# A third pair of operand tiles, a raw ring of three, and a copy of the sums' high part in PSUM, in the down projection of a decoder step

## The chip, the cores and the metric

The kernel runs on one core of one Trainium2 chip. The metric is device time in microseconds. Three runs of the kernel before gave a median of 3109.16 us (3107.42 to 3110.7).

## What is computed

One decoder layer for 512 prompt tokens and 8 sample tokens that share weights (T = 520 columns): a mixer (RG-LRU and gated DeltaNet), cross-attention and a SwiGLU, each with a norm before and after. The change is in the last product of the last part:

```python
def swiglu(xn, p):
    return (jax.nn.silu(xn @ p['ffn_w_gate']) * (xn @ p['ffn_w_up'])) @ p['ffn_w_down']
```

D_MODEL is 2048 and D_FF is 5632, so `ffn_w_down` is 44 x 16 blocks of 128 x 128, all in fp32.

## The kernel before

**Split operands.** Each fp32 operand is split into a high part (a copy to fp32r, made by ScalarE) and a low part (the operand minus its high part, made by VectorE). A product is three matmuls: high with high, high with low, low with high.

**Seven products.** The two feed-forward stages use Strassen's scheme: 2 x 2 blocks of weight against 2 x 2 blocks of tokens (halves of 260 columns) in seven products, collected in PSUM banks 0 to 6. Bank 7 is not used by them. A *slab* is a tile of weight: raw blocks A11, A12, A21, A22 for two pairs, `raw[k]` of 128 x 1024. Of it, three blocks are operands as they are (w_hi and w_lo, planes 0 to 5), and four sums (`w_sums`, later `down_sums`, 128 x 1024) give planes 6 to 13. TensorE takes a slab in 7 x 2 x 3 = 42 matmuls of 260 columns (`products`, L3770 to L3791).

**The down phase.** UP = 176 slabs of the up projection come first; then 88 slabs of down, in four parts of 12, 12, 12 and 8 chunks of D_FF (PARTS). A part has eight *units*, one for each 256 output columns; a unit is three slabs in the first three parts and two in the fourth. At a unit's end VectorE adds the seven banks up (`combine`, L2942 to L2954, four instructions), and the result goes to `ffn_out`: copied by ScalarE in the first part (`copy_out`, L1908), added by GpSimd in the second and third (`add_out`, L1028), added by VectorE in the fourth (L3032), where ScalarE also squares and weighs it (`square_out`, L1921 and L1926) and GpSimd adds the squares (L1037). Towards the end of the first three parts, six, six and two of the hidden activations' sets are loaded from memory and split (`set_high_down` L1897, `set_low_down` L3021), in pairs after a slab.

**What each engine does for slab n**, in a fixed order that is the order of the code:

- SyncE loads raw[n % 4] when slab n-4 has its low part (`load_down`, L1134).
- GpSimd makes the sums of slab n in three instructions (`down_sum`, L1016, L1019, L1021) once slab n-2 has its low part; two buffers take turns.
- ScalarE copies the raw blocks (L1880) and then the sums (L1883) to w_hi. `down_high` waits for `w_used >= n - 1`: TensorE must be done with slab n-2, since two tiles take turns.
- VectorE subtracts: L3012 for the raw blocks, L3015 for the sums, and counts `w_low` up.
- TensorE waits for `w_low` and multiplies.

On ScalarE, `first_product` (L1840) follows the high part of the next unit's first slab; on VectorE, `combine` follows the low part of the same slab.

Of the kernel before, what the change touches and what calls it, by code (L numbers as in the profile page):

```python
# [12 lines left out]
P = 128  # L13
# [48 lines left out]
def build(nc, i, o):  # L62
# [32 lines left out]
    with ExitStack() as ctx:  # L95
        def sb(name, shape, dt=F32):
# [12 lines left out]
                       ("qs_rows", 4), ("k_t", NC // 2), ("s_exp", 1), ("os_rows", 1), ("s_o_high", 1), ("xa_root", 1), ("y_copied", Y_TILES)],  # L109
# [6 lines left out]
                       ("s_probs", 1), ("s_spread", 1), ("s_o_low", 1), ("s_ssum", 1), ("xa_mean", 1), ("last_added", 2), ("y_first", 1), ("y_made", Y_TILES)],  # L116
# [229 lines left out]
        assert EARLY + 2 * HALF_SLOT <= SET  # L346
        FIRST_TILES = (0, 1, 4, 1)
# [14 lines left out]
        ffn_out = at("ffn_out", [P, NC, T], F32, SUMS0)  # L362
        assert SUMS0 + CH <= LATER + 4 * HALF_SLOT
# [89 lines left out]
        ps = ctx.enter_context(nc.psum_tensor("ps", [P, 8, 512], F32))  # L453

# [95 lines left out]
        assert all(n + 1 <= used_at(kp) for n, kps in SET_AT.items() for kp in kps)  # L550

# [191 lines left out]
        def _(pool):  # L743
# [264 lines left out]
            def down_sum(n):  # L1008

                raw_, t = raw[n % 4], sums_of(n)  # L1010
                pool.wait_ge(sem(f"raw_loaded{n % 4}"), 32 * (n // 4 + 1))
# [47 lines left out]
        def _(sp):  # L1059
# [133 lines left out]
        def _(act):  # L1193
# [779 lines left out]
        def _(dve):  # L1973
# [1128 lines left out]
        def _(pe):  # L3102
# [699 lines left out]
            for p, (c0, cn) in enumerate(PARTS):  # L3802
                ns, slots = cn // KS, [(c0 // 2 + j) % KP for j in range(cn // 2)]
                for v in range(2):
                    products(PART_SLAB[p] + v * ns, [(v * ns + s) % 2 for s in range(ns)], FF + p * DB + v, slots, fresh=c0 // 2 if v == 0 else None)
                with pe.Fori(1, DB // 2) as it:
                    for v in range(2):
                        products(it * (2 * ns) + (PART_SLAB[p] + v * ns), [(v * ns + s) % 2 for s in range(ns)], it * 2 + (FF + p * DB + v), slots)
# [56 lines left out]
```

## Time and profile before

| | us |
|---|---|
| median of three runs | 3109.16 |
| lowest, highest | 3107.42, 3110.7 |
| the profiled execution, its own time | 3109.38 |
| span of its trace | 3107.8 |
| granted TensorE clock, mean | 0.984 |

The span runs from the first to the last instruction; the execution's own time is 1.6 us more. TensorE is at its peak when a slab of 42 matmuls takes about 5.0 us, so a unit of three slabs 15 and one of two 10. A matmul's record is longer than its share, since matmuls overlap. Where an engine's record overlaps the next one's, the distance between starts is what the engine gives to it. [...]

### The profile page before, as it was taken

The numbers are of one execution on the slowest core, as the hardware profiler recorded it, in microseconds if no ns is written. First come the engines' busy times: TensorE is split into PE (matmuls) and PEld (weight loads), VectorE is DVE, ScalarE is ACT, GpSimd is POOL, SyncE is SP. The second block draws the span as 40 slices with busy tenths as digits, with TensorE's granted clock in tenths as the row PEclk, the third lists the DMA queues.
The fourth block names the chain that finished last, engine by engine and source line by source line (L and its number), as shares of the span: only waits on it lengthen the run. The fifth ranks groups of instructions, "written<-read, shape, count | busy, mean of one in ns | idle before, by whom it ended". The sixth has DMA issues, their size and how long they took to land.

```text
span 3107.8 us, 60002 instructions
## 1 busy us (share of the span) xinstructions
PE 2983.0 (96%) x23609; PEld 2862.4 (92%) x23609; DVE 2166.2 (70%) x2876; ACT 1345.7 (43%) x2037; POOL 710.6 (23%) x588
## 2 busy tenths in 40 slices
PE   8999999999999999999997999999999998998988
PEld 6789999998889999978797999999999998988988
DVE  4544336454665477565368999999999987788788
ACT  5442443334364555333355344343434444534344
POOL 0000000001353000010000122222211126678885
PEclk9999999999999999999998999999999999999999
DMA  7553223232216457886664444444444453424333
GB/s 275 181 179 110 81 77 95 88 95 71 69 42 218 160 194 245 287 317 237 236 203 136 131 126 128 127 132 125 121 129 126 126 186 116 167 88 154 102 106 144
DMA packets 457580, 460.56 MB, mean 148 GB/s; under 512 B 22619, under 2 KB 420988, under 8 KB 449551
## 3 DMA queue, kind: packets, MB, share of 16 engines
q1 hardware_dynamic: 436778, 357.88, 36.7%
q0 software_dynamic: 11712, 69.55, 5.9%
q10 hardware_dynamic: 8944, 31.12, 2.7%
q8 instruction: 99, 1.62, 0.2%
q14 instruction: 47, 0.39, 0.0%
HBM read 416.00 MB, written 42.74 MB: 148 GB/s over the span
## 4 chain that ended last, share of the span: by engine, by line
PE 78%; DVE 13%; ACT 3%; DMA 2%; issue 2%; POOL 1%; ACTq 0%; DVEq 0%; SPq 0%; POOLq 0%
PE ps L3180 16%; PE ps L3589 16%; PE ps L3786 12%; PE ps L3788 11%; PE ps L3787 11%; PE ps L3177 5%; DVE w_lo L3015 3%; DVE w_lo L3012 1%; DVE w_low L2033 1%; DVE set_low L3021 1%; ACT w_high L1215 1%; DMA w_raw<-in_xa_wo 1%; PE ps L3680 1%; DVE prods L2954 1%; DMA q_wide<-q_mid 1%
## 5 line engine op out<-in xcount | busy, mean ns | idle before, releaser
L3786 PE MATMUL ps<-set_high,w_hi 128*128 128x260 f32 x3584 | 1025.5, 286 | 56.4 <-DVE w_lo L3015 38.7
L3788 PE MATMUL ps<-set_high,w_lo 128*128 128x260 f32 x3584 | 1022.2, 285 | 0.0
L3787 PE MATMUL ps<-set_low,w_hi 128*128 128x260 f32 x3584 | 1022.1, 285 | 0.0
L2033 DVE TENSOR_TENSOR w_low<-w_raw,w_high 128x1024 fp32r<-128x1024 f32 x354 | 434.8, 1229 | 623.0 <-ACT w_high L1215 622.4
L3786 PEld LDWEIGHTS ps<-set_high,w_hi 128*128 128x128 f32 x3584 | 684.8, 191 | 64.2 <-DVE w_lo L3015 44.4
L3788 PEld LDWEIGHTS ps<-set_high,w_lo 128*128 128x128 f32 x3584 | 685.6, 191 | 0.0
L3787 PEld LDWEIGHTS ps<-set_low,w_hi 128*128 128x128 f32 x3584 | 684.0, 191 | 0.0
L1215 ACT ACTIVATE w_high<-w_raw 128x1024 fp32r<-128x1024 f32 x356 | 377.1, 1060 | 642.3 <-PE ps L3589 298.3
L1779 ACT ACTIVATE w_hi<-raw 128x768 fp32r<-128x768 f32 x168 | 142.4, 847 | 468.6 <-PE ps L3788 468.6
L3180 PE MATMUL ps<-x_high,w_high 128*128 128x260 f32 x1568 | 318.8, 285 | 2.6 <-DVE w_low L2033 2.4
L3180 PE MATMUL ps<-x_low,w_high 128*128 128x260 f32 x1568 | 314.5, 282 | 0.0
L3180 PE MATMUL ps<-x_high,w_low 128*128 128x260 f32 x1568 | 314.0, 282 | 0.0
L3589 PE MATMUL ps<-x_high,w_high 128*128 128x264 f32 (+1 forms) x1024 | 296.7, 290 | 8.7 <-DVE w_low L2033 8.6
L3589 PE MATMUL ps<-x_low,w_high 128*128 128x264 f32 (+1 forms) x1024 | 291.8, 285 | 0.0
L3589 PE MATMUL ps<-x_high,w_low 128*128 128x264 f32 (+1 forms) x1024 | 291.4, 285 | 0.0
L997 POOL TENSOR_TENSOR h_sums<-h_out,h_out 128x260 f32<-128x260 f32 x22 | 90.0, 4092 | 873.0 <-DVE h_out L2979 873.0
L3180 PEld LDWEIGHTS ps<-x_high,w_high 128*128 128x128 f32 x1568 | 240.7, 188 | 8.9 <-issue 4.8
L3180 PEld LDWEIGHTS ps<-x_low,w_high 128*128 128x128 f32 x1568 | 241.6, 188 | 0.0
L3180 PEld LDWEIGHTS ps<-x_high,w_low 128*128 128x128 f32 x1568 | 241.1, 188 | 0.0
L2873 DVE TENSOR_TENSOR w_lo<-w_sums,w_hi 128x1024 fp32r<-128x1024 f32 x168 | 216.0, 1286 | 0.0
L2866 DVE TENSOR_TENSOR w_lo<-raw,w_hi 128x768 fp32r<-128x768 f32 x168 | 170.3, 1014 | 65.1 <-ACT w_hi L1779 63.4
L3589 PEld LDWEIGHTS ps<-x_high,w_high 128*128 128x128 f32 x1024 | 195.8, 191 | 20.1 <-issue 18.1
(560 smaller groups left out, 5375.6 us busy)
## 6 DMA issues: line engine op xcount, KB each, us to landing
w_raw<-in_w_in SPq DMA_DIRECT2D x96, 512.0 KB
raw<-in_ffn_w_up SPq DMA_DIRECT2D x176, 256.0 KB, 2.9
raw<-in_ffn_w_gate SPq DMA_DIRECT2D x176, 256.0 KB, 3.2
raw<-in_ffn_w_down SPq DMA_DIRECT2D x176, 256.0 KB, 3.0
w_raw<-in_w_out SPq DMA_DIRECT2D x64, 512.0 KB
w_raw<-in_xa_wq SPq DMA_DIRECT2D x64, 512.0 KB
w_raw<-in_xa_wo SPq DMA_DIRECT2D x64, 512.0 KB
set_raw<-h_mid ACTq DMA_DIRECT2D x22, 910.0 KB, 6.9
```

The costliest lines, as they stand in the source:

```text
L1215: act.activation(w_high[:, slot], w_raw[:, (g.slab0 + jj) % RAW], ACT.Copy).then_inc(sem("w_high_ready"), 1)
L1779: act.activation(w_hi[k][:, 0:6].rearrange("p (a b) c -> p a (b c)", a=2), raw[k][:, :, 1:4].rearrange("p a b c -> p a (b c)"), ACT.Copy). ...
L2033: dve.tensor_tensor(w_low[:, slot], w_raw[:, (g.slab0 + jj) % RAW], w_high[:, slot].bitcast(F32), ALU.subtract).then_inc(sem("w_low_ready" ...
L2866: dve.tensor_tensor(lo[:, 0:6].rearrange("p (a b) c -> p a (b c)", a=2), raw[k][:, :, 1:4].rearrange("p a b c -> p a (b c)"), hi[:, 0:6].b ...
L2873: dve.tensor_tensor(lo[:, 6:14], sums[:].rearrange("p s a c -> p (s a) c"), hi[:, 6:14].bitcast(F32), ALU.subtract).then_inc(sem("w_low"), 1)
L3015: dve.tensor_tensor(w_lo[k][:, 6:14], sums_of(n)[:].rearrange("p s a c -> p (s a) c"), w_hi[k][:, 6:14].bitcast(F32), ALU.subtract).then_i ...
L3177: ins = pe.matmul(ps[:, b + 2 * m, 0:g.width], x[:, c, m * P:(m + 1) * P], g.slab_of(w, slot)[:, k], **flags)
L3180: ins = pe.matmul(ps[:, b + 2 * m + h, 0:HALF], wk, x[:, c, h * HALF:(h + 1) * HALF], **flags)
L3589: ins = pe.matmul(ps[:, b + m, 0:g.tokens.stop - g.tokens.start], w[:, slot, k, m * P:(m + 1) * P], x[:, c0 + k, g.tokens], start=c0 + k = ...
L3786: pe.matmul(ps[:, bank, 0:HALF], high, set_high[:, kp, x], start=s + half == 0, stop=False)
L3787: pe.matmul(ps[:, bank, 0:HALF], high, set_low[:, kp, x], start=False, stop=False)
L3788: ins = pe.matmul(ps[:, bank, 0:HALF], low, set_high[:, kp, x], start=False, stop=s == len(tiles) - 1 and half == 1)
```

## The change

1. **Tiles.** One more pair of tiles exists, w_hi5 and w_lo5; `down_tile(n)` lets three pairs take turns (tiles 0, 1 and 5; tile 3 once). ScalarE's copy of the raw blocks waits for `w_used >= n - 2` in place of `n - 1`.
2. **Raw ring.** Room for that comes from the raw ring, which has three slots in the down phase in place of four. `load_down` waits for `w_low >= n - 2` in place of `n - 3`. `ffn_out` moves to another address.
3. **Sums.** ScalarE copies the sums also to PSUM bank 7 (`sum_high`, 512 columns), half by half, and VectorE subtracts bank 7 from the sums, half by half, in place of w_hi's planes 6 to 13. The copy of the whole sums to w_hi stays.
4. **Order.** Slab 1 of the down phase gets its low part before the first set, and TensorE's loop over the units of a part (after the first two, which stand ahead of it) takes two units of three slabs to a pass, or three of two, so that the tiles repeat.

```diff
+        w_hi.append(at("w_hi5", [P, 14, P], F32R, RAW0 + 3 * SLAB))
+        w_lo.append(at("w_lo5", [P, 14, P], F32R, H_OUT))
...
+        sum_high = ps[:, 7].rearrange("p (b c) -> p b c", c=P).bitcast(F32R)
...
+        def down_tile(n):
+
+            d = (n - UP) % 3
+            return d if d < 2 else 3 if n == UP + 2 else 5
...
             def load_down(n):
                 p, v, n0, _ = [u for u in UNITS if u[2] <= n][-1]
-                sp.wait_ge(sem("w_low"), n - 3)
+                sp.wait_ge(sem("w_low"), n - (3 if n < UP + 3 else 2))
...
+            def high_sums(n, half):
+
+                if half:
+                    act.wait_ge(sem("down_summed"), 3 * (n - UP) + 3)
+                    act.wait_ge(*after("sums_low", n - UP + 1))
+                else:
+                    act.wait_ge(sem("down_summed"), 3 * (n - UP) + 1)
+                    if n > UP:
+                        act.wait_ge(sem("w_low"), n)
+                act.activation(sum_high, sums_of(n)[:, 2 * half:2 * half + 2].rearrange("p s a c -> p (s a) c"), ACT.Copy).then_inc(sem("sums_high"), 1)
+
             def down_high(n):
 
-                k = n % 2
-                act.wait_ge(sem("w_used"), n - (3 if n < UP + 2 else 1))
-                act.wait_ge(sem(f"raw_loaded{n % 4}"), 32 * (n // 4 + 1))
-                act.activation(w_hi[k][:, 0:6].rearrange("p (a b) c -> p a (b c)", a=2), raw[n % 4][:, :, 1:4].rearrange("p a b c -> p a (b c)"),
+                k = down_tile(n)
+                act.wait_ge(*down_loaded(n))
+                high_sums(n, 0)
+                act.wait_ge(sem("w_used"), n - (3 if n < UP + 2 else 2))
...
+                act.activation(w_hi[k][:, 0:6].rearrange("p (a b) c -> p a (b c)", a=2), down_raw(n)[:, :, 1:4].rearrange("p a b c -> p a (b c)"),
                                ACT.Copy).then_inc(sem("w_high"), 1)
-                act.wait_ge(sem("down_summed"), 3 * (n - UP) + 3)
+                high_sums(n, 1)
                 act.activation(w_hi[k][:, 6:14], sums_of(n)[:].rearrange("p s a c -> p (s a) c"), ACT.Copy).then_inc(sem("w_high"), 1)
...
+            def low_sums(n, half):
+
+                dve.wait_ge(*after("sums_high", 2 * (n - UP) + half + 1))
+                return dve.tensor_tensor(w_lo[down_tile(n)][:, 6 + 4 * half:10 + 4 * half], sums_of(n)[:, 2 * half:2 * half + 2].rearrange("p s a c -> p (s a) c"),
+                                         sum_high.bitcast(F32), ALU.subtract)
+
             def down_low(n):
 
-                k = n % 2
+                k = down_tile(n)
                 dve.wait_ge(sem("w_high"), 2 * n + 1)
...
+                low_sums(n, 0).then_inc(sem("sums_low"), 1)
                 dve.wait_ge(sem("w_high"), 2 * n + 2)
-                dve.tensor_tensor(w_lo[k][:, 6:14], sums_of(n)[:].rearrange("p s a c -> p (s a) c"), w_hi[k][:, 6:14].bitcast(F32),
-                                  ALU.subtract).then_inc(sem("w_low"), 1)
+                low_sums(n, 1).then_inc(sem("w_low"), 1)
```

ScalarE's queue at the second unit of the first part, before. The names in brackets are the semaphores that an instruction waits for; `prods<-ps` is `first_product`.

```order
L1880 ACTIVATE w_hi_197<-raw_191 128x768 [waits raw_loaded1,w_used]
L1883 ACTIVATE w_hi_197<-down_sums_228 128x1024 [waits down_summed]
L1880 ACTIVATE w_hi_196<-raw_192 128x768 [waits raw_loaded2,w_used]
L1883 ACTIVATE w_hi_196<-down_sums_227 128x1024 [waits down_summed]
L1840 ACTIVATE prods<-ps 128x260 [waits done]
```

And the same queue after the change, two slabs:

```order
L1902 ACTIVATE ps<-down_sums_229 128x512 [waits w_low,down_summed,raw_loaded0]
L1914 ACTIVATE w_hi_196<-raw_190 128x768 [waits w_used]
L1902 ACTIVATE ps<-down_sums_229 128x512 [waits vector_steps,down_summed]
L1917 ACTIVATE w_hi_196<-down_sums_229 128x1024
...
L1902 ACTIVATE ps<-down_sums_230 128x512 [waits w_low,down_summed,raw_loaded1]
L1914 ACTIVATE w_hi_197<-raw_191 128x768 [waits w_used]
L1902 ACTIVATE ps<-down_sums_230 128x512 [waits vector_steps,down_summed]
L1917 ACTIVATE w_hi_197<-down_sums_230 128x1024
```

Two copies to `ps` (bank 7) have joined each slab; the first waits for `w_low`, which VectorE counts, and the second for `vector_steps`, which VectorE counts after the first half (`sums_low`).

VectorE's queue around a unit's end, before:

```order
L3012 TENSOR_TENSOR w_lo_200<-raw_192,w_hi_196 128x768 [waits w_high]
L3015 TENSOR_TENSOR w_lo_200<-down_sums_227,w_hi_196 128x1024 [waits w_high]
L2945 TENSOR_TENSOR prods<-ps,prods 128x2x260 [waits first_copied,done,out_taken]
L2948 TENSOR_TENSOR prods<-ps,prods 128x260 [waits combined,done]
L2951 TENSOR_TENSOR prods<-ps,prods 128x520 [waits combined,done]
L2954 TENSOR_TENSOR prods<-ps,prods 128x520 [waits combined,w_used]
L3012 TENSOR_TENSOR w_lo_201<-raw_193,w_hi_197 128x768 [waits w_high]
```

And after:

```order
L3052 TENSOR_TENSOR w_lo_200<-raw_190,w_hi_196 128x768 [waits w_high]
L3045 TENSOR_TENSOR w_lo_200<-down_sums_229,ps 128x512 [waits scalar_steps]
L3045 TENSOR_TENSOR w_lo_200<-down_sums_229,ps 128x512 [waits scalar_steps,w_high]
L2979 TENSOR_TENSOR prods<-ps,prods 128x2x260 [waits first_copied,done,out_taken]
L2982 TENSOR_TENSOR prods<-ps,prods 128x260 [waits combined,done]
L2985 TENSOR_TENSOR prods<-ps,prods 128x520 [waits combined,done]
L2988 TENSOR_TENSOR prods<-ps,prods 128x520 [waits combined,w_used]
L3052 TENSOR_TENSOR w_lo_201<-raw_191,w_hi_197 128x768 [waits w_high]
```

One subtraction of 1024 elements has become two of 512 that read `ps`; each waits for ScalarE (`scalar_steps` counts `sums_high`), and the second also for the copy of the whole sums (`w_high`).

## Rows read from the trace of the kernel before

**Rows 1.** The page, its first line.

```profile
span 3107.8 us, 60002 instructions
```

**Rows 2.** Busy time by stretch of the down phase: PE, PEld, DVE, ACT, POOL, PEclk, DMA.

```profile
2592.00:2682.00 90.00, 89.99 (x748) 89.78 (x749) 59.96 (x61) 39.39 (x48) 54.19 (x56) 1.00 0.32 106
2682.00:2724.00 42.00, 35.39 (x265) 34.63 (x264) 35.88 (x27) 25.03 (x24) 28.02 (x19) 0.90 0.57 208
2724.00:2822.00 98.00, 92.91 (x746) 91.89 (x746) 76.77 (x59) 32.15 (x40) 79.46 (x60) 0.97 0.30 97
2822.00:2867.00 45.00, 36.19 (x266) 34.99 (x265) 41.22 (x28) 22.77 (x22) 36.27 (x21) 0.92 0.52 195
2867.00:2965.00 98.00, 91.09 (x749) 89.83 (x748) 77.38 (x61) 32.38 (x41) 80.47 (x61) 1.00 0.30 97
2965.00:2998.00 33.00, 28.51 (x213) 27.91 (x212) 27.57 (x21) 12.62 (x14) 25.91 (x17) 0.90 0.40 136
2998.00:3071.00 73.00, 63.42 (x491) 62.20 (x490) 69.18 (x55) 37.52 (x54) 67.71 (x47) 0.95 0.38 131
```

**Rows 3.** Who waited for whom, 2540 to 3090: us in total, times, longest.

```profile
ACT w_hi L1880 <- PE ps L3788: 271.5, 78, 9.5
...
PE ps L3786 <- DVE w_lo L3015: 38.7, 26, 7.2
```

**Rows 4.** Timeline, first part: start, us, engine, line, operation, [idle before].

```profile
2627.79 0.85 ACT L1880 ACTIVATE w_hi<-raw 128x768 fp32r<-128x768 f32 x1 [2.27 <-PE ps L3788]
2628.54 1.04 ACT L1883 ACTIVATE w_hi<-down_sums 128x1024 fp32r<-128x1024 f32 x1
...
2621.13 0.68 DVE L2945 TENSOR_TENSOR prods<-ps,prods 128x520 f32<-128x520 f32 x1
...
2623.87 1.21 DVE L3012 TENSOR_TENSOR w_lo<-raw,w_hi 128x768 fp32r<-128x768 f32 x1
...
2628.67 1.42 DVE L3012 TENSOR_TENSOR w_lo<-raw,w_hi 128x768 fp32r<-128x768 f32 x1 [2.45 <-ACT w_hi L1880]
2630.02 1.21 DVE L3015 TENSOR_TENSOR w_lo<-down_sums,w_hi 128x1024 fp32r<-128x1024 f32 x1
...
2628.54 0.74 POOL L1021 TENSOR_TENSOR down_sums<-raw,down_sums 128x256 f32<-128x256 f32 x1
2631.37 1.29 POOL L1016 TENSOR_TENSOR down_sums<-raw 128x512 f32<-128x512 f32 x1 [2.09 <-DVE w_lo L3015]
```

**Rows 5.** Timeline, third part: VectorE and GpSimd where both run.

```profile
2903.14 3.44 DVE L3015 TENSOR_TENSOR w_lo<-down_sums,w_hi 128x1024 fp32r<-128x1024 f32 x1
...
2902.36 3.14 POOL L1028 TENSOR_TENSOR ffn_out<-ffn_out,prods 128x1040 f32<-128x1040 f32 x1
```

**Rows 6.** Groups of instructions by line; one by duration min/median/max.

```profile
L1333 ACT ACTIVATE qkv<-conved 128x512 f32<-128x512 f32 (+1 forms) x24 | 15.0, 627 | 47.2 <-DVE conved L2081 47.2
...
L1897 ACT ACTIVATE set_high<-set_raw 128x1820 fp32r<-128x1820 f32 x19 | 32.0, 1712 | 2.5 <-DMA set_raw<-h_mid 2.5
...
L3015 DVE TENSOR_TENSOR w_lo<-down_sums,w_hi 128x1024 fp32r<-128x1024 f32 x86 | 180.5, 2099 | 6.8 <-ACT w_hi L1883 6.8
...
L3021 DVE TENSOR_TENSOR set_low<-set_raw,set_high 128x1820 fp32r<-128x1820 f32 x20 | 49.6, 2513 | 0.8 <-ACT set_high L1897 0.8
L2954 DVE TENSOR_TENSOR prods<-ps,prods 128x520 f32<-128x520 f32 x32 | 22.4, 700 | 4.6 <-PE ps L3788 1.5
...
L2979 DVE TENSOR_TENSOR h_out<-prods x44: 687/692/705, 1700.4 to 2568.6; 128x520 f32<-128x520 f32 x44
```

**Rows 7.** Timeline, fourth part: the extra work of its units.

```profile
3038.30 1.17 ACT L1921 ACTIVATE out_sq<-ffn_out 128x520 f32<-128x520 f32 x2 [0.21 <-DVE ffn_out L3032]
3039.37 1.34 ACT L1926 ACTIVATE ffn_out<-ffn_out,par 128x520 f32<-128x520 f32 x2
...
3037.03 1.24 DVE L3032 TENSOR_TENSOR ffn_out<-ffn_out,prods 128x1040 f32<-128x1040 f32 x1
...
L1037 POOL TENSOR_TENSOR out_ssum<-out_ssum,out_sq x13: 1310/2093/2101, 3003.6 to 3077.9; 128x520 f32<-128x520 f32 x13
```

More of the change, by code:

```diff
@@ L346, in build @@
         assert EARLY + 2 * HALF_SLOT <= SET
+        w_hi.append(at("w_hi5", [P, 14, P], F32R, RAW0 + 3 * SLAB))
+        w_lo.append(at("w_lo5", [P, 14, P], F32R, H_OUT))
+        FFN_OUT = (RAW0 + 3 * SLAB + HALF_SLOT + 992) // 32 * 32
+        assert H_OUT + HALF_SLOT <= SET
         FIRST_TILES = (0, 1, 4, 1)
@@ L361, in build @@
         s_ssum = at("s_ssum", [P, B], F32, X_IN + 4 * TB + NC * B * 4)
-        ffn_out = at("ffn_out", [P, NC, T], F32, SUMS0)
-        assert SUMS0 + CH <= LATER + 4 * HALF_SLOT
+        ffn_out = at("ffn_out", [P, NC, T], F32, FFN_OUT)
+        assert FFN_OUT + CH <= nc.sbuf_usable_end
         LAST = 2 * SLOT // TB
@@ L550, in build, with down_raw, down_loaded @@
         assert all(n + 1 <= used_at(kp) for n, kps in SET_AT.items() for kp in kps)
+        def down_tile(n):
+            d = (n - UP) % 3
+            return d if d < 2 else 3 if n == UP + 2 else 5
+        def down_raw(n):
+            return raw[(n - UP) % 3]
+        def down_loaded(n):
+            return sem(f"raw_loaded{(n - UP) % 3}"), 32 * (UP // 4 + (n - UP) // 3 + 1)
         def sums_of(n):
@@ L1008, in down_sum @@
             def down_sum(n):
-                raw_, t = raw[n % 4], sums_of(n)
-                pool.wait_ge(sem(f"raw_loaded{n % 4}"), 32 * (n // 4 + 1))
+                raw_, t = down_raw(n), sums_of(n)
+                pool.wait_ge(*down_loaded(n))
                 pool.wait_ge(sem("w_low"), max(n - 1, UP))
@@ L1136, in load_down @@
                 p, v, n0, _ = [u for u in UNITS if u[2] <= n][-1]
-                sp.wait_ge(sem("w_low"), n - 3)
+                sp.wait_ge(sem("w_low"), n - (3 if n < UP + 3 else 2))
                 c = PARTS[p][0] + KS * (n - n0)
                 for a in range(2):
-                    sp.dma_start(raw[n % 4][:, a].rearrange("p (b m) c -> p b (m c)", b=2),
-                                 down_rows[:, c + 2 * a:c + 2 * a + 2, v * COLS:(v + 1) * COLS]).then_inc(sem(f"raw_loaded{n % 4}"), 16)
+                    sp.dma_start(down_raw(n)[:, a].rearrange("p (b m) c -> p b (m c)", b=2),
+                                 down_rows[:, c + 2 * a:c + 2 * a + 2, v * COLS:(v + 1) * COLS]).then_inc(down_loaded(n)[0], 16)
             def store_h(j, k):
@@ L1873, in _ @@
                 up_unit(u)
-            def down_high(n):
-                k = n % 2
-                act.wait_ge(sem("w_used"), n - (3 if n < UP + 2 else 1))
-                act.wait_ge(sem(f"raw_loaded{n % 4}"), 32 * (n // 4 + 1))
-                act.activation(w_hi[k][:, 0:6].rearrange("p (a b) c -> p a (b c)", a=2), raw[n % 4][:, :, 1:4].rearrange("p a b c -> p a (b c)"),
+            def high_sums(n, half):
[7 more added lines that the diff above has]
+                act.activation(sum_high, sums_of(n)[:, 2 * half:2 * half + 2].rearrange("p s a c -> p (s a) c"), ACT.Copy).then_inc(sem("sums_high"), 1)
+            def down_high(n):
+                k = down_tile(n)
+                act.wait_ge(*down_loaded(n))
+                high_sums(n, 0)
+                act.wait_ge(sem("w_used"), n - (3 if n < UP + 2 else 2))
+                if n == UP + 5:
+                    for h in range(2):
+                        act.wait_ge(sem(f"h_stored{h}"), 16 * HP)
+                    act.wait_ge(sem("h_sums_stored"), 32 * HP)
+                act.activation(w_hi[k][:, 0:6].rearrange("p (a b) c -> p a (b c)", a=2), down_raw(n)[:, :, 1:4].rearrange("p a b c -> p a (b c)"),
                                ACT.Copy).then_inc(sem("w_high"), 1)
-                act.wait_ge(sem("down_summed"), 3 * (n - UP) + 3)
+                high_sums(n, 1)
                 act.activation(w_hi[k][:, 6:14], sums_of(n)[:].rearrange("p s a c -> p (s a) c"), ACT.Copy).then_inc(sem("w_high"), 1)
@@ L3060, in _ @@
             down_low(UP)
+            down_low(UP + 1)
             set_low_down(0)
-            down_low(UP + 1)
             set_low_down(1)
@@ L3804, in _ @@
                 for v in range(2):
[L3805 to L3808, printed above, removed]
+                    n0 = PART_SLAB[p] + v * ns
+                    products(n0, [down_tile(n0 + s) for s in range(ns)], FF + p * DB + v, slots, fresh=c0 // 2 if v == 0 else None)
+                m = 2 if ns == 3 else 3
+                assert m * ns % 3 == 0 and (DB - 2) % m == 0
+                with pe.Fori(0, (DB - 2) // m) as it:
+                    for v in range(2, 2 + m):
+                        n0 = PART_SLAB[p] + v * ns
+                        products(it * (m * ns) + n0, [down_tile(n0 + s) for s in range(ns)], it * m + (FF + p * DB + v), slots)
             def y_turned(which, a):
```

6 lines of the change are left out of this document (3 added, 3 removed).

## The prediction

> **What bounds the kernel now.** I read the stretches first, then the waits, then the timelines. The span is 3107.8 us [rows 1]; the profiled execution took 3109.38, 0.2 above the median of 3109.16, so the sum is made against 3109.4 and holds for the median. The change touches the last 560 us only. I cut that phase where VectorE begins to add a unit's banks, so that each stretch of [rows 2] holds whole units: six units of the first part; two around its end, where sets are loaded; six of the second part; two around its end; six of the third; its end with the fourth's start; six of the fourth. The reader should see three regimes. In the first stretch TensorE is busy for 89.99 of 90 us: 15.0 us a unit, its peak. In the two other long ones a unit takes 98/6 = 16.3, and TensorE idles 5 to 7 us in each. In the fourth part a unit of two slabs takes 73/6 = 12.2 against 10.0. In all, TensorE waits 38.7 us for VectorE's low part of the sums [rows 3]: the prize. ScalarE, which feeds VectorE, waits 271.5 us for TensorE to give a tile back [rows 3], and this wait the third pair loosens.
>
> What stretches the low part: its 1024 elements take 1.21 us in the first part [rows 4], 3.44 where GpSimd adds to ffn_out at that time [rows 5], 2.10 in the mean of 86 [rows 6]. In [rows 4] the raw blocks' 768 elements take 1.42 where GpSimd's L1021 runs until 2629.28. That looks as if one of the two engines stood while the other reads two operands from SBUF. VectorE's additions that read PSUM show none of it: 0.70 in the mean of 32 for 520 elements [rows 6], beside the same GpSimd work.
>
> **The new cycle.** What decides is not a duration but who waits for whom. Bank 7 is one buffer with two uses per slab. ScalarE's first half-copy waits until the slab before is finished on VectorE (w_low >= n); the second waits for VectorE's first half; VectorE's second half waits for ScalarE's whole copy, behind the second half-copy in the queue. So the seven steps of a slab follow each other, and nothing of slab n+1 begins before slab n ends. Before, ScalarE's two copies of the next slab ran beside VectorE's work, and only TensorE's use of the tile held them.
>
> Durations for a slab, from the end of the last low part as 0. Handover ScalarE to VectorE: 2627.79 + 0.85 to 2628.67 is 0.03 [rows 4], taken for both directions. Consecutive copies start 0.10 before the end of the one in front (0.85 long, next start 0.75 later) [rows 4], subtractions 0.07.
>
> - First half-copy, 512 elements: no row has ScalarE writing PSUM. The nearest copies 512 from SBUF to SBUF in 0.627 [rows 6]. Bounds: 0.52, half the 1.04 of 1024 elements, and 0.75. I take 0.63. It runs 0.03 to 0.66.
> - Raw copy 0.85 [rows 4]: 0.56 to 1.41.
> - Raw low part, 768 elements: 1024 take 1.21 [rows 4] and 520 take 0.69 (L2979) [rows 6], so 1.03 ns each, 0.95 here: 1.44 to 2.39. GpSimd's L1016 starts 0.14 after a low part ends (2630.02 + 1.21 to 2631.37) and takes 1.29 [rows 4], so ends at 1.43, just in time. Bounds 0.95 and 1.42.
> - First half low: PSUM is read by the additions at 0.70 for 520 [rows 6], and 0.70 I take: 2.32 to 3.02. Bounds 0.60 (half of 1.21) and 0.76.
> - Second half-copy: 3.05; the whole copy follows at 3.58 and takes 1.04, to 4.62. Second half low: 4.65 to 5.35.
>
> A cycle is **5.35 us**, against 5.0 that TensorE needs (90 us for 18 slabs). At a unit's end `combine` stands between two slabs. It takes 2623.87 - 2621.13 = 2.74 on VectorE [rows 4]; meanwhile ScalarE does its first 1.4 us. The raw low part then starts at 2.74, takes 1.21 as at 2623.87, and the rest 2.96, to 6.91. A three-slab unit takes 6.91 + 2 x 5.35 = **17.6 us**. GpSimd's add_out lies beside it at no cost, as halves from PSUM don't meet it.
>
> [...] The rows show 0.69 (L2979) and 0.70 (L2954) for 520 elements [rows 6], so almost no difference. [...]
>
> **The sum, by stretch** [rows 2]:
>
> - Three long stretches of three-slab units: 18 x 17.6 = 317 against 90 + 98 + 98 = 286: **+31**. In the first TensorE was the bound, so all of 2.6 a unit is new.
> - Ends of the first two parts. A slab with a pair of sets: from the raw low's start, 3.18 to the end of the whole copy, then set_high 1.71 and two set_lows of 2.51 [rows 6], of which the first starts when one set_high is done: 3.08 + 1.71 + 0.03 + 5.02 = 9.84 to the next slab. First unit: 17.6 + 9.84 - 3.91 = 23.5; second, with two pairs: 2.74 + 2 x 9.84 + 3.91 = 26.3. Together 49.8 against 42 and 45: **+13**.
> - End of the third part: 23.5 + one unit of two slabs (6.91 + 5.35) = 35.8 against 33: **+3**.
> - Fourth part. After `combine` VectorE adds to ffn_out: starts at 2.87, 1.24 long [rows 7], with some of L1021 in the way ends at 4.3. Slab one: raw low 4.2 to 5.15, then 2.96: 8.1. ScalarE's squares and weights come after its whole copy, at 7.3, and take 3038.30 to 3040.71 = 2.4 [rows 7], to 9.7. Only then begins slab two's cycle: 5.3 more to its low part's end, and 0.6 because GpSimd, whose two additions of 1.3 at best [rows 7] end at 10.5, is at its sums when the raw low comes: 15.6. Six units 94 against 73: **+21**.
> - Start: the first three slabs have the longer chain too (5.35 against 0.75 + 1.04 + 0.03 + 1.21 = 3.03 from raw copy to low part [rows 4]), two of them on the path to the first sets: 2 x 2.3 = **+4.6**. Bounds 0 (hidden behind the set loads) and 8.
> - Removed waits: none is kept. TensorE's release of a tile stops being the wait, but bank 7's comes later than it. The load of a raw slab now starts one cycle later; 5.3 us remain for it before GpSimd asks for it, so at nothing; if a load took over 5.3 it would push the sums, which have one more cycle as cover.
> - The other loop on TensorE, the moved ffn_out: nothing, in TensorE's queue the same 3696 matmuls.
>
> 31 + 13 + 3 + 21 + 4.6 = 72.6, so **3182 us**, 2.3% slower.
>
> **Rivals.**
>
> *A, faster: the chain is shorter than I make it and TensorE bounds.* For: the PSUM halves take the 2.10 us low part to 1.40, and the third pair removes ScalarE's 271.5 us of waiting. Against: the waits of the queue listing. It decides where the cycle, combine shared over three slabs, falls to about 5.0: 17.6 must fall to 15.0, 0.87 a slab, more than the low bounds of both halves and both half-copies give together (0.4). Then the second and third parts give 2 x (98 - 90) = 16, the fourth 73 - 60 = 13: 3080. The point of no change is a cycle of about 4.5. [...]
>
> [...]
>
> *C, milder: the ends and the fourth part don't grow.* There VectorE is full already (69.18 of 73 us) [rows 2], and each slab of it loses up to 0.8 us of stretched low part. If this work, not the chain, is the bound, those stretches stay: 72.6 - 13 - 3 - 21 = 36, so 3145.
>
> *D, no change*: VectorE's relief and the chain just cancel: 3109. Nothing speaks for it but the size of the terms.
>
> **How the numbers follow.** Forecast 0.66, A 0.05, B 0.12, C 0.12, D 0.05. The unknown half-copies (0.52 to 0.75), the raw low part (0.95 to 1.42) and the reads of PSUM (0.60 to 0.76) move a cycle by -0.4 to +0.8, of which I take a third to be likely: 88 slabs by -0.13 to +0.35 is -12 to +31. With B and C inside the range is 3145 to 3216. A measurement of this kernel can tell 0.2%, about 6 us, from no change: faster 0.05, same 0.05, slower 0.90.
>
> **What would show it.** Right: VectorE's halves 0.70 each, the same in all four parts; ScalarE's first half-copy released by VectorE in nearly each slab, no longer by TensorE; TensorE idle some 0.3 us before each slab and near 2 at each unit, 17.6 us a unit in the first part where it was 15.0; 15.6 in the fourth. Wrong: a first stretch still at 15.0 a unit with TensorE full; or a half-copy starting before the low part in front has ended.

## The result

The changed kernel took **3187.04 us** in the median of four runs (3186.34 to 3194.5), the kernel before 3108.69 in the same comparison: a ratio of 1.0258, 95% interval 1.0243 to 1.0273, so slower by 2.6%. The profiled execution of the changed kernel took 3194.5 us, 7.5 more than the median and 7.2 more than any of the other three, and the stretches below are of that one.

The page of the changed kernel:

```profile
span 3192.9 us, 60442 instructions
...
PE 3007.9 (94%) x23609; PEld 2876.4 (90%) x23609; DVE 2095.2 (66%) x2964; ACT 1443.8 (45%) x2213; POOL 688.8 (22%) x588
...
PEclk9999999999999999999999999999999989898989
```

The same line on the page of before:

```profile
PE 2983.0 (96%) x23609; PEld 2862.4 (92%) x23609; DVE 2166.2 (70%) x2876; ACT 1345.7 (43%) x2037; POOL 710.6 (23%) x588
```

VectorE and GpSimd are busy for 71 and 22 us less than before, and ScalarE for 98 us more. The span is 85 us longer than in [rows 1]. TensorE has the same matmuls and sits idle between them.

Busy time by stretch, cut at the same units as [rows 2]; columns PE, PEld, DVE, ACT, POOL, granted clock, DMA share, GB/s:

```profile
2598.80:2708.70 109.90, 96.84 (x756) 93.20 (x756) 59.03 (x80) 59.80 (x84) 58.63 (x54) 0.98 0.27 86
2708.70:2760.20 51.50, 36.40 (x252) 35.10 (x252) 34.84 (x33) 29.36 (x34) 28.29 (x18) 0.87 0.47 170
2760.20:2867.90 107.70, 96.65 (x756) 92.94 (x756) 56.64 (x79) 54.70 (x78) 78.00 (x60) 0.98 0.27 88
2867.90:2919.40 51.50, 35.42 (x252) 34.18 (x252) 34.84 (x34) 27.55 (x32) 34.50 (x20) 0.87 0.47 170
2919.40:3026.30 106.90, 96.85 (x756) 93.12 (x756) 56.12 (x80) 54.72 (x78) 78.32 (x60) 0.98 0.27 89
3026.30:3062.50 36.20, 28.88 (x204) 27.98 (x205) 21.57 (x27) 18.39 (x24) 25.80 (x17) 0.86 0.36 125
3062.50:3156.00 93.50, 72.87 (x512) 70.63 (x510) 53.80 (x68) 50.07 (x78) 51.37 (x48) 0.89 0.31 108
```

| stretch | before | forecast | after |
|---|---|---|---|
| up to the first unit's additions | 2591.8 | +4.6 | 2598.8, +7.0 |
| six units, first part | 89.5 | 105.6 | 109.9 |
| end of the first part, two units | 41.9 | 49.8 | 51.5 |
| six units, second part | 98.8 | 105.6 | 107.7 |
| end of the second part | 44.5 | 49.8 | 51.4 |
| six units, third part | 98.2 | 105.6 | 106.9 |
| end of the third part, two units | 33.1 | 35.8 | 36.2 |
| six units, fourth part | 73.1 | 94 | 93.5 |

Before and after are distances between VectorE's first addition (L2945 before, L2979 after) of the units at the ends. The differences, start included, sum to 85 us, the whole of what the profiled execution lost (3194.5 - 3109.4). The largest lie in the first part (20.4 us), where TensorE had been full at all times and is busy for 96.84 of 109.9 us now, and in the fourth (20.4 us).

Who waited for whom, 2540 to 3170 (us in total, times, longest):

```profile
ACT ps L1902 <- DVE w_lo L3045: 253.7, 141, 6.8
DVE w_lo L3045 <- ACT w_hi L1917: 150.7, 88, 2.0
POOL down_sums L1034 <- DVE w_lo L3045: 150.6, 75, 5.4
DVE w_lo L3052 <- ACT w_hi L1914: 93.0, 52, 6.4
PE ps L3826 <- DVE w_lo L3045: 90.5, 76, 8.4
```

ScalarE waits for VectorE now, 141 times of 176 half-copies; before, it waited 271.5 us for TensorE [rows 3]. VectorE waits for ScalarE in turn, once in each of 88 slabs. TensorE's wait for the low part has grown from 38.7 to 90.5 us.

One slab of the first part, without its neighbours: the seven steps in ScalarE's and VectorE's timelines (start, us, engine, line, operation):

```profile
2648.18 0.60 ACT L1902 ACTIVATE ps<-down_sums 128x512 fp32r<-128x512 f32 x1 [0.83 <-DVE w_lo L3045]
2648.72 0.83 ACT L1914 ACTIVATE w_hi<-raw 128x768 fp32r<-128x768 f32 x1
2651.23 0.60 ACT L1902 ACTIVATE ps<-down_sums 128x512 fp32r<-128x512 f32 x1 [1.68 <-DVE w_lo L3045]
2651.77 1.05 ACT L1917 ACTIVATE w_hi<-down_sums 128x1024 fp32r<-128x1024 f32 x1
...
2647.38 0.69 DVE L3045 TENSOR_TENSOR w_lo<-down_sums,ps 128x512 fp32r<-128x512 f32 x1 [1.71 <-ACT w_hi L1917]
2649.58 0.96 DVE L3052 TENSOR_TENSOR w_lo<-raw,w_hi 128x768 fp32r<-128x768 f32 x1 [1.51 <-ACT w_hi L1914]
2650.45 0.68 DVE L3045 TENSOR_TENSOR w_lo<-down_sums,ps 128x512 fp32r<-128x512 f32 x1
2652.84 0.69 DVE L3045 TENSOR_TENSOR w_lo<-down_sums,ps 128x512 fp32r<-128x512 f32 x1 [1.71 <-ACT w_hi L1917]
```

From the end of one low part (2647.38 + 0.69 = 2648.07) to the next (2652.84 + 0.69 = 2653.53) it is 5.46 us. First half-copy, raw copy, raw low part, first half low, second half-copy, whole copy, second half low: each begins 0.02 to 0.11 us after the end of what it waits for, or behind its predecessor on its own engine. Of these seven steps no two lie side by side, but for the overlap at the seams.

Durations, minimum, median and maximum:

```profile
L3045 DVE TENSOR_TENSOR w_lo<-down_sums,ps x172: 672/685/690, 2585.3 to 3163.3; 128x512 fp32r<-128x512 f32 x172
...
L1902 ACT ACTIVATE ps<-down_sums x172: 576/602/604, 2583.0 to 3161.7; 128x512 fp32r<-128x512 f32 x172
```

The half low from PSUM takes 0.67 to 0.69 us in all 172 cases, in each part, with GpSimd at work or idle. The low part of the sums took 2.10 us in the mean before [rows 6]; two halves take 1.37.

### The profile page after: what moved, and what is told of

Its sections match the earlier page's. It is cut to its first block, busy times and chain, and to the rows that moved or that the text cites. A ratio compares the mean times of both kernels' runs of the same rounds, so it can differ in the third digit from the quotient of the medians.

```text
span 3192.9 us, 60442 instructions
## 1 busy us (share of the span) xinstructions
PE 3007.9 (94%) x23609; PEld 2876.4 (90%) x23609; DVE 2095.2 (66%) x2964; ACT 1443.8 (45%) x2213; POOL 688.8 (22%) x588
## 3 DMA queue, kind: packets, MB, share of 16 engines
q1 hardware_dynamic: 436778, 357.88, 35.8%
q8 instruction: 100, 1.64, 0.2%
## 4 chain that ended last, share of the span: by engine, by line
PE 70%; DVE 15%; ACT 9%; issue 2%; DMA 2%; POOL 0%; ACTq 0%; DVEq 0%; SPq 0%; POOLq 0%
PE ps L3220 16%; PE ps L3629 16%; PE ps L3826 9%; PE ps L3828 9%; PE ps L3827 9%; PE ps L3217 4%; DVE w_lo L3052 3%; DVE w_lo L3045 3%; ACT w_hi L1917 3%; ACT ps L1902 2%; DVE set_low L3061 1%; ACT w_hi L1914 1%; DVE w_low L2067 1%; ACT w_high L1233 1%; DVE prods L2985 1%
## 5 line engine op out<-in xcount | busy, mean ns | idle before, releaser
L3826 PE MATMUL ps<-set_high,w_hi 128*128 128x260 f32 x3584 | 1035.9, 289 | 116.2 <-DVE w_lo L3045 90.5
L3220 PEld LDWEIGHTS ps<-x_high,w_high 128*128 128x128 f32 x1568 | 240.7, 188 | 9.0 <-issue 4.8
L1902 ACT ACTIVATE ps<-down_sums 128x512 fp32r<-128x512 f32 x172 | 103.1, 600 | 283.6 <-DVE w_lo L3045 249.5
```

What stands on the lines that cost most here:

```text
L1902: act.activation(sum_high, sums_of(n)[:, 2 * half:2 * half + 2].rearrange("p s a c -> p (s a) c"), ACT.Copy).then_inc(sem("sums_high"), 1)
L3220: ins = pe.matmul(ps[:, b + 2 * m + h, 0:HALF], wk, x[:, c, h * HALF:(h + 1) * HALF], **flags)
L3826: pe.matmul(ps[:, bank, 0:HALF], high, set_high[:, kp, x], start=s + half == 0, stop=False)
```

## Experiments

Each was compared with the kernel before on the same chip. They ran on several chips, on which the kernel before took 3106.0 to 3108.7, so a difference of 3 us between experiments on different chips shows nothing. Unit times are averages over the six units of a long stretch, as above. Of the changed kernel they are 18.3 in the first part, 17.9 and 17.8 in the second and third, 15.6 in the fourth; of the kernel before 14.9, 16.5, 16.4, 12.2. A value a little below TensorE's 15.0 means that VectorE's additions moved closer to TensorE within the stretch.

### One part of the change at a time

**e1_third_pair**: the third pair and the raw ring of three, without bank 7.

```diff
-                high_sums(n, 0)
...
-                high_sums(n, 1)
+                act.wait_ge(sem("down_summed"), 3 * (n - UP) + 3)
...
-                low_sums(n, 0).then_inc(sem("sums_low"), 1)
                 dve.wait_ge(sem("w_high"), 2 * n + 2)
-                low_sums(n, 1).then_inc(sem("w_low"), 1)
+                dve.tensor_tensor(w_lo[k][:, 6:14], sums_of(n)[:].rearrange("p s a c -> p (s a) c"), w_hi[k][:, 6:14].bitcast(F32),
+                                  ALU.subtract).then_inc(sem("w_low"), 1)
```

> The changed kernel with its three tile pairs and its raw ring of three, but without bank 7: the sums' low part is one subtraction from w_hi again, as before the change. Theory (the chain through bank 7 is the whole loss; what bounded the second to fourth parts before is that VectorE and GpSimd take turns at SBUF, which a third pair does not help): 3095 to 3110, first-part units 15.0, units of the second part about 16. Rival 1 (the ring of three loads too late and costs): above 3130. Rival 2 (the wait for TensorE's tile was the bound before): the second and third parts fall to 15.0 a unit, about 3080.

Measured: 3095.94 us, ratio 0.9964 (0.995 to 0.9978), so 11 us faster than before. Units 14.7, 15.8, 15.7, 12.4. The whole loss is gone with bank 7. The ring of three costs nothing that shows beside the gain; no run has the third pair with a ring of four, so its price alone is not measured. The third pair helps a little, above all in the second and third parts. What holds these at 15.8 and 15.7 in place of 15.0 is new, as the waits and GpSimd's timeline of the second part have it:

```profile
ACT w_hi L1916 <- POOL down_sums L1039: 198.5, 63, 11.1
...
2765.34 1.29 POOL L1034 TENSOR_TENSOR down_sums<-raw 128x512 f32<-128x512 f32 x1
2766.70 1.61 POOL L1037 TENSOR_TENSOR down_sums<-raw,down_sums 128x256 f32<-128x256 f32 x1
2768.39 0.74 POOL L1039 TENSOR_TENSOR down_sums<-raw,down_sums 128x256 f32<-128x256 f32 x1
2769.08 1.30 POOL L1034 TENSOR_TENSOR down_sums<-raw 128x512 f32<-128x512 f32 x1
2770.46 0.73 POOL L1037 TENSOR_TENSOR down_sums<-raw,down_sums 128x256 f32<-128x256 f32 x1
2771.27 1.35 POOL L1039 TENSOR_TENSOR down_sums<-raw,down_sums 128x256 f32<-128x256 f32 x1
2772.57 3.42 POOL L1046 TENSOR_TENSOR ffn_out<-ffn_out,prods 128x1040 f32<-128x1040 f32 x1
```

ScalarE waits 198.5 us for the sums now, and GpSimd works without a gap: seven instructions follow each other from 2765.34 to 2775.99. The same instruction takes 1.61 in one slab and 0.73 in the next (L1037), or 0.74 and 1.35 (L1039). VectorE subtracts two SBUF operands when the L1037 of 1.61 (from 2766.49 to 2767.72) and the L1039 of 1.35 start (until 2772.01); at the L1039 of 0.74 it adds from PSUM. At the L1037 of 0.73 GpSimd starts 0.02 us ahead of VectorE's subtraction, and keeps its time. The time came out in the theory's range (3095 to 3110), but a third pair does help somewhat, which the theory had denied.

**e2_two_pairs**: bank 7 kept, two tile pairs.

```diff
-            d = (n - UP) % 3
-            return d if d < 2 else 3 if n == UP + 2 else 5
+            return (n - UP) % 2
...
-                act.wait_ge(sem("w_used"), n - (3 if n < UP + 2 else 2))
+                act.wait_ge(sem("w_used"), n - (3 if n < UP + 2 else 1))
```

> The changed kernel with bank 7 and both half-copies, but two tile pairs taking turns, and ScalarE's raw copy waiting for w_used >= n - 1 as before the change. Theory (the chain through bank 7 sets the pace, so that the third pair never matters): within 10 us of the changed kernel's 3187, a first-part unit still near 18.4. Rival (the third pair gives back something that bank 7 costs): 3205 or more.

Measured: 3191.53 us, ratio 1.0267 (1.025 to 1.0284); units 18.5, 18.1, 17.9, 15.6. As the theory has it: with the chain through bank 7 in place, a third pair gives back 3 to 5 us of 80, and the two intervals overlap.

### The chain, link by link

**e5_after_twice**: a link made longer.

```diff
+                if not half:
+                    act.activation(sum_high, sums_of(n)[:, 2 * half:2 * half + 2].rearrange("p s a c -> p (s a) c"), ACT.Copy).then_inc(sem("sums_high"), 1)
+                    act.wait_ge(*after("sums_high", 3 * (n - UP) + 1))
                 act.activation(sum_high, sums_of(n)[:, 2 * half:2 * half + 2].rearrange("p s a c -> p (s a) c"), ACT.Copy).then_inc(sem("sums_high"), 1)
```

(VectorE's counts follow.)

> The changed kernel with ScalarE's first half-copy to bank 7 made twice per slab, the second time waiting for the first. Theory (that copy is a link of the chain): 0.65 us more in each slab that does not stand behind a unit's additions or a pair of sets, where ScalarE has time to spare; some 50 of 88, so +33 us, about 3220. Rival (ScalarE's work lies beside TensorE's and costs nothing): within 5 us of 3187.

Measured: 3215.63 us, ratio 1.0353 (1.0335 to 1.037), 29 us above the changed kernel's 3187. The two copies stand one behind the other on ScalarE:

```profile
2649.23 0.60 ACT L1903 ACTIVATE ps<-down_sums 128x512 fp32r<-128x512 f32 x1 [0.83 <-DVE w_lo L3048]
2649.87 0.60 ACT L1905 ACTIVATE ps<-down_sums 128x512 fp32r<-128x512 f32 x1
2650.40 0.83 ACT L1917 ACTIVATE w_hi<-raw 128x768 fp32r<-128x768 f32 x1
2652.91 0.60 ACT L1905 ACTIVATE ps<-down_sums 128x512 fp32r<-128x512 f32 x1 [1.68 <-DVE w_lo L3048]
2653.45 1.04 ACT L1920 ACTIVATE w_hi<-down_sums 128x1024 fp32r<-128x1024 f32 x1
...
2655.33 0.60 ACT L1903 ACTIVATE ps<-down_sums 128x512 fp32r<-128x512 f32 x1 [0.56 <-DVE w_lo L3048]
```

From one first copy to the next (2649.23 to 2655.33) it is 6.10 us, against 5.47 in the changed kernel (2648.18 to 2653.65): the added 0.64 is passed on in full. Units are 19.1 in each of the first three parts and 15.7 in the fourth. In the second and third that is 1.1 and 1.3 more: the two slabs of a unit that don't stand behind additions grow from 5.47 to 6.10 each, and the third stays at 6.88, since ScalarE has time there. In the first part it is only 0.8 more, since its third slab was at 6.06 before and is at 6.11 now (more of this slab below, under the first part). In the fourth part it is 0.1 more: VectorE's 1.8 us for the second slab's raw blocks (L3052) in the changed kernel is 1.2 here, which takes most of the added time up.

**e3_whole_first**: a link taken out by order alone.

```diff
+                act.wait_ge(sem("down_summed"), 3 * (n - UP) + 3)
+                act.activation(w_hi[k][:, 6:14], sums_of(n)[:].rearrange("p s a c -> p (s a) c"), ACT.Copy).then_inc(sem("w_high"), 1)
                 high_sums(n, 1)
-                act.activation(w_hi[k][:, 6:14], sums_of(n)[:].rearrange("p s a c -> p (s a) c"), ACT.Copy).then_inc(sem("w_high"), 1)
```

> The changed kernel with ScalarE's copy of the whole sums moved ahead of its second half-copy, nothing else. The whole copy then runs beside VectorE's raw low part and first half and leaves the chain: a cycle of about 4.4 us in place of 5.35. Theory (the chain): first-part units at TensorE's 15.0, second and third part 15.0, fourth part 13 to 13.5, in all 3095 to 3110. Rival (the loss is ScalarE's added work or slow reads of bank 7, not the order of the steps): above 3160.

Measured: 3108.2 us, ratio 1.0001 (0.9992 to 1.0011): two instructions in another order give back all 79 us. Units 15.1, 15.1, 15.1, 13.8. VectorE's timeline of the first part:

```profile
2648.79 0.69 DVE L3046 TENSOR_TENSOR w_lo<-down_sums,ps 128x512 fp32r<-128x512 f32 x1 [0.80 <-ACT ps L1902]
2650.99 0.96 DVE L3053 TENSOR_TENSOR w_lo<-raw,w_hi 128x768 fp32r<-128x768 f32 x1 [1.52 <-ACT w_hi L1914]
2651.87 0.68 DVE L3046 TENSOR_TENSOR w_lo<-down_sums,ps 128x512 fp32r<-128x512 f32 x1
2653.35 0.69 DVE L3046 TENSOR_TENSOR w_lo<-down_sums,ps 128x512 fp32r<-128x512 f32 x1 [0.80 <-ACT ps L1902]
```

From the end of one slab's low part (2648.79 + 0.69) to the next (2653.35 + 0.69) it is 4.56 us, below TensorE's 5.0 (4.4 expected). The slab behind additions takes 5.98, so that a unit is 5.98 + 2 x 4.56 = 15.10, in all three parts: the loop still sets the pace here, 0.1 above TensorE. The same instructions, ScalarE's added copies and the reads of bank 7 among them, cost next to nothing in the long stretches once one of them has left the line. The gain of the second and third parts (1.4 and 1.3 us a unit) is spent again at the ends (46.2 and 46.1 in place of 41.9 and 44.5) and in the fourth part.

### What the parts are worth without the chain

**e4_one_half**: only the first half goes through bank 7.

```diff
                     if n > UP:
-                        act.wait_ge(sem("w_low"), n)
+                        act.wait_ge(*after("sums_low", n - UP))
...
-                high_sums(n, 1)
+                act.wait_ge(sem("down_summed"), 3 * (n - UP) + 3)
...
-                dve.wait_ge(*after("sums_high", 2 * (n - UP) + half + 1))
+                dve.wait_ge(*after("sums_high", n - UP + 1))
...
-                low_sums(n, 1).then_inc(sem("w_low"), 1)
+                dve.tensor_tensor(w_lo[k][:, 10:14], sums_of(n)[:, 2:4].rearrange("p s a c -> p (s a) c"), w_hi[k][:, 10:14].bitcast(F32),
+                                  ALU.subtract).then_inc(sem("w_low"), 1)
```

> Only the first half of the sums goes through bank 7; the second half's low part is taken from w_hi, so one half-copy a slab falls away, and the first half-copy waits only for VectorE's first half of the slab in front. ScalarE can be a slab ahead of VectorE. Theory (the chain): no cycle over TensorE's 5.0 remains; first part 15.0, second and third part 15.0 (VectorE's time at SBUF falls by a half), fourth part 11 to 12, in all 3080 to 3095, below both kernels. Rival (bank 7 itself is slow or ScalarE too busy): above 3110.

Measured: **3076.62 us**, ratio 0.9902 (0.9885 to 0.9918). Units 14.7, 15.0, 15.0, 11.3; ends 40.7, 42.8, 30.1. It is faster than both kernels, and 3 us below the expected range. It holds the cleanest measurement of how the low part is stretched beside GpSimd, since both halves have the same 512 elements and differ in where the high part is read: PSUM in L3045, SBUF in L3056 (minimum, median, maximum):

```profile
L3045 DVE TENSOR_TENSOR w_lo<-down_sums,ps x86: 671/675/682, 2578.7 to 3042.4; 128x512 fp32r<-128x512 f32 x86
...
L3056 DVE TENSOR_TENSOR w_lo<-down_sums,w_hi x86: 675/1176/2348, 2579.3 to 3043.0; 128x512 fp32r<-128x512 f32 x86
```

At the least they take 0.67 and 0.68. The one that reads PSUM stays there, and the other takes 1.18 in the median and 2.35 at most. **e10_one_half_again**, the same kernel once more:

> The kernel with one half through bank 7 once more, on the same chip as the one before, so that the two are compared side by side: 3075 to 3079, and clearly below the kernel before the change (3107).

Measured: 3075.66 us, ratio 0.99 (0.9884 to 0.9917).

**e6_one_half_twice**: the doubling of e5 in this kernel.

> The same doubling in the kernel that sends only the first half through bank 7 (3077 us), where ScalarE is no link of a closed chain. Theory: 0 to +8 us, 3077 to 3085. Rival (ScalarE's copies cost wherever they stand): +33 as in the other, 3110.

Measured: 3081.24 us, ratio 0.9924 (0.9908 to 0.9941), 5 us above e4, on another chip and with intervals that overlap. The same added copies cost 29 us in the chain and at most some 5 outside of it.

**e9_one_half_two_pairs**: the edit of e2 in this kernel.

> The kernel with one half through bank 7 (3077 us) with two tile pairs in place of three. Theory (once the chain is gone, the wait for TensorE's tile counts again, above all behind the ends and in the fourth part): 3085 to 3095. Rival (the third pair is worth nothing, the relief of SBUF is all): 3077, within 3 us.

Measured: 3087.66 us, ratio 0.9946 (0.9929 to 0.9963), 11 us above e4, with intervals that don't overlap: the third pair is worth 11 us here, as it was in e1 against the kernel before. Units 14.8, 15.2, 15.7, 11.3, read from an execution of 3081.63, which is 6 us below the other three. With two pairs one half in bank 7 is worth 19 us against the kernel before.

**e7_one_half_raw_first**: raw copy ahead of the half-copy.

```diff
-                high_sums(n, 0)
                 act.wait_ge(sem("w_used"), n - (3 if n < UP + 2 else 2))
...
                                ACT.Copy).then_inc(sem("w_high"), 1)
+                high_sums(n, 0)
```

> The kernel with one half through bank 7 (3077 us), with ScalarE's raw copy ahead of its half-copy, so that neither VectorE's finished half nor GpSimd's first sum holds the raw copy up. Theory (no closed chain is left, ScalarE has slack; only units of the fourth part and the ends can gain): 3070 to 3077. Rival (the half-copy's wait, now behind the raw copy, comes later for VectorE, whose first half follows its raw low part by 0.9 us only): 3080 to 3085.

Measured: 3074.8 us, ratio 0.99 (0.9884 to 0.9917). Beside e10 on the same chip it is 0.9 us less, which these runs can't tell apart. Units 14.7, 15.0, 15.0, 11.2.

**e8_whole_and_raw_first**: e3 and the edit of e7 together, both halves through bank 7.

> Both halves through bank 7 as in the change, but ScalarE's order in a slab is raw copy, first half-copy, whole copy, second half-copy. Of the seven steps only the first half-copy, the first half low, the second half-copy and the second half low follow each other: 0.6 + 0.7 + 0.6 + 0.7 and handovers, about 2.8 us. Theory (the chain, and apart from it VectorE's and GpSimd's turns at SBUF, of which both halves are free here): 15.0 in the first three parts, 11 or less in the fourth, 3060 to 3075. Rival (with the chain gone ScalarE's 3.1 us a slab and the handovers still hold the fourth part and the ends): 3085 to 3110.

Measured: 3097.08 us, ratio 0.9971 (0.9961 to 0.9982): above what I expected by 20 us, and inside the range of the rival, by which ScalarE's work still holds the fourth part and the ends (3085 to 3110). Units 14.9, 14.9, 14.9, 13.1; ends 46.1, 45.9, 29.6. The first three long stretches are at TensorE's pace, and the rest is not. Two engines in the fourth part:

```profile
3013.03 0.60 ACT L1902 ACTIVATE ps<-down_sums 128x512 fp32r<-128x512 f32 x1 [4.34 <-DVE w_lo L3046]
3013.57 1.15 ACT L1956 ACTIVATE out_sq<-ffn_out 128x520 f32<-128x520 f32 x2
3014.62 1.33 ACT L1961 ACTIVATE ffn_out<-ffn_out,par 128x520 f32<-128x520 f32 x2
3015.86 0.83 ACT L1913 ACTIVATE w_hi<-raw 128x768 fp32r<-128x768 f32 x1
...
3012.26 0.68 DVE L3046 TENSOR_TENSOR w_lo<-down_sums,ps 128x512 fp32r<-128x512 f32 x1
3013.74 0.69 DVE L3046 TENSOR_TENSOR w_lo<-down_sums,ps 128x512 fp32r<-128x512 f32 x1 [0.80 <-ACT ps L1902]
3016.73 1.12 DVE L3053 TENSOR_TENSOR w_lo<-raw,w_hi 128x768 fp32r<-128x768 f32 x1 [2.30 <-ACT w_hi L1913]
```

The second half-copy (3013.03) waits for VectorE's first half (3012.26 + 0.68), and behind it in ScalarE's queue stand the squares and weights, 2.4 us, and then the next raw copy, for which VectorE waits from 3014.43 to 3016.73. The squares could have begun at 3010.93, when VectorE's addition to `ffn_out` ends (L3073); they begin 2.6 us later. The sets at the ends stand behind that half-copy too. In e4, where only one half goes through bank 7, no half-copy stands in front of the squares, and they begin 0.04 us after VectorE's addition ends (2996.51 to 2996.55), beside its low parts. I had counted the links and left out what is queued behind a link.

## Why the prediction was right

**The forecast** of a chain that closes through bank 7 held in mechanism, place and size: 3182 against 3187. The waits turned round as it said, and the seven steps stand in line in the trace. No half-copy of the 88 first ones starts before the low part in front has ended, which would have been the sign of being wrong. That the total came within 5 us is in part luck: the forecast is made against the profiled execution of before, and the profiled one of after took 12.5 more than 3182. By stretch the down phase took some 11 us more than forecast, as the next paragraphs have it.

**The cycle**: 5.35 forecast, 5.46 measured. The half-copy takes 0.60, not 0.63; no row had shown a write to PSUM by ScalarE, and the 0.63 was that of another line's copies from SBUF to SBUF, with fp32 output [rows 6]. What I had wrong was the handover from VectorE to ScalarE, set to 0.03 like the one back: it is 0.11 and 0.10 (2648.07 to 2648.18, 2651.13 to 2651.23), twice a slab. The slab behind `combine` came to 6.89 us (2653.53 to 2660.42), forecast 6.91.

**The read of PSUM**: 0.685 us in the median for 512 elements, near the row's 0.70 for 520. Of my two bounds 0.60 was half of a row, and 0.76 stands in no row and no run: the halves took 0.67 to 0.69. Of the two lines whose times the prediction sets side by side, L2979 (0.69) has both operands in SBUF and L2954 (0.70) has one in PSUM. In e4 it is as close: the same 512 elements take 0.671 us at least with one source in PSUM and 0.675 with both in SBUF.

**The first part** came to 18.3 a unit, not 17.6: 4.3 us in the stretch, the largest miss of a term. The longer handovers are 0.2 of it in each unit (6.88 + 2 x 5.47 = 17.8), as in the other two long stretches. The other 0.5 is one slab of the three. Behind `copy_out` (L1942 now) ScalarE's next half-copy starts 0.14 us after the low part's end (2641.32 + 0.69 = 2642.01) in place of 0.11:

```profile
2641.19 1.05 ACT L1942 ACTIVATE ffn_out<-prods 128x1040 f32<-128x1040 f32 x1
2642.15 0.58 ACT L1902 ACTIVATE ps<-down_sums 128x512 fp32r<-128x512 f32 x1
...
2643.53 1.54 DVE L3052 TENSOR_TENSOR w_lo<-raw,w_hi 128x768 fp32r<-128x768 f32 x1 [1.53 <-ACT w_hi L1914]
...
2643.52 0.74 POOL L1037 TENSOR_TENSOR down_sums<-raw,down_sums 128x256 f32<-128x256 f32 x1
```

The raw low part then starts at 2643.53, 0.01 us after GpSimd's L1037, and takes 1.54 in place of 0.96, which makes the slab 6.06 us long in place of 5.47. In the slab shown before, both start at 2649.58 and VectorE goes first: 0.96, and it is L1037 that takes 1.55. The trace has 43 slabs in which the two start within 0.02 us of each other. In 7 of them GpSimd is ahead by 0.006 us or more, and the raw low part takes 1.53 to 1.55; in the other 36 it takes 0.96. Six of the seven are in the first part and one is in the second, whose units are 17.9 against 17.8 in the third. That is the "just in time" of the forecast: a race that a hundredth of a microsecond decides. The forecast had the lost race among its bounds (0.95 and 1.42 for the raw low part), but its 17.6 put it at nothing.

**The ends and the fourth part**: 51.5 and 51.4 against 49.8, 36.2 against 35.8, 93.5 against 94. Most of the miss at the first two ends is again the raw low part: behind a pair of sets it took 1.48 and 1.49 in place of 0.95. In the fourth part the parts of the sum came out too: in the unit that begins at 3093.29 the first slab's low part ends at 8.0 us (forecast 8.1), the squares and weights at 9.6 (9.7), and the second slab's low part at 15.7 (15.6). The second slab's raw low part meets GpSimd's sums, as forecast, for 0.9 us in place of 0.6:

```profile
3104.17 1.84 DVE L3052 TENSOR_TENSOR w_lo<-raw,w_hi 128x768 fp32r<-128x768 f32 x1 [2.86 <-ACT w_hi L1914]
...
3103.91 1.29 POOL L1034 TENSOR_TENSOR down_sums<-raw 128x512 f32<-128x512 f32 x1
```

Rival C, which let these stretches stay as they were, is refuted: VectorE is busy for 53.80 of 93.5 us in the fourth part, where it had been for 69.18 of 73 [rows 2]. Before, its L3015 took 1.64 to 2.33 us there, against 1.21 at the least in the trace; with that time gone the chain took its place.

**The start**: +7.0 in the profiled execution, forecast +4.6. Of the 7.0, 2.7 have nothing to do with the change: at the additions of the last up unit but one VectorE is 2.7 us later already (2539.7 against 2537.0), and it is just as much later 800 us earlier (1734.1 against 1731.4). From there to the first unit's additions it takes 59.1 us, where it took 54.8: +4.3, so the term was right. e2 has 59.2 for it. What the other 5 of the 7.5 us are, by which this execution is longer than the median, stays open, as the other three have no trace.

**Rival A** (TensorE bounds): refuted, and e3 shows its point of decision: with a cycle of 4.56 us, close to the 4.5 that the prediction gave as the point of no change, the ratio is 1.0001. It is a balance of stretches, though: the first part, the first two ends and the fourth part are longer than before, the others shorter.

**Rival B**, 0.12 of the chances, was a granted TensorE clock that stays at half of full speed through the fourth part, and the range up to 3216 takes it in. No run shows such a clock (the lowest mean over those 94 us is 0.87, in e2): in the changed kernel it fell to 0.89 in the fourth part (1.00 is full speed), from 0.95, and to 0.86 and 0.87 at the ends. It did fall to 0.50, but in short stretches and not throughout. In the unit above TensorE sat idle for 2.5 us until 3093.42, and 1.2 us later the clock was at 0.50 for 3.3 us (the row of that stretch, columns as above):

```profile
3094.60:3097.90 3.30, 3.30 (x18) 3.30 (x17) 3.16 (x4) 0.17 (x1) 1.60 (x3) 0.50 0.46 153
```

The clock set no pace: the waits from 2600 to 3160 have no instruction of ScalarE or VectorE that waited for TensorE, and TensorE was idle for 20 us of the fourth part.

**The raw ring of three** at nothing: held, as far as the runs show. GpSimd waited for a load in 3 cases, 7.2 us, in the changed kernel, and in none before. e1 with the same ring is faster than the kernel before, with the third pair's gain in it.

What the prediction did not see is how close the change was to a gain. Without the chain, one half in bank 7 is worth 19 us (e9), the third pair 11 us (e1), and both together 31 us (e4): the two add up.

## What to carry to other kernels

A single buffer that two engines hand to each other twice per step closes a loop: add up its links before you look at busy times, since an engine that is busy for half the time can still be in it. Then see which links are there only because of an engine's queue order; here, moving one copy ahead of another was worth 79 us. And look at what is queued behind the waiting instruction: in e8 that, not the loop, set the fourth part.

## What the runs showed of the hardware

- VectorE's subtraction of two SBUF operands was stretched, up to 2.348 us, where GpSimd's sums and additions fell beside it, and the same subtraction with one operand in PSUM was not: 1.176 against 0.675 us in the median for the same 512 elements in one kernel (e4). I had expected the latter from the additions, but not that the one with PSUM would be so free of scatter (0.671 to 0.682). The nine with two SBUF operands that had no GpSimd instruction beside them took 0.677 to 0.685.
- The stretch went both ways. Where VectorE's L3052 and GpSimd's L1037 started within 0.02 us of each other, L3052 took 0.96 us and L1037 1.54 to 1.56 in the 36 cases in which VectorE was ahead, or behind by at most 0.005 us, and L3052 1.53 to 1.55 and L1037 0.73 to 0.74 in the 7 in which GpSimd was ahead by 0.006 us or more (the changed kernel).
- A handover from VectorE to ScalarE took 0.09 to 0.12 us, from ScalarE to VectorE 0.03, from VectorE to GpSimd 0.14 to 0.15 (the changed kernel).
- ScalarE's copy of 512 fp32 from SBUF to PSUM took 0.60 us; another line's copy of 512 from SBUF to SBUF, with fp32 output, took 0.63 [rows 6].
- After TensorE had been idle for 2.5 us and busy for 1.2, its granted clock was 0.50 of full speed for 3.3 us (the changed kernel, fourth part).
